# Second attention's last steps: values of the second sample group ahead of the turns, and an output projection begun early

## The reference

```python
outs, lses = [], []
for g, (win, dil) in enumerate(((128, 1), (512, 4), (2048, 16))):   # three dilation groups, 8 heads
    o_g, l_g = dilated(q[:, :, g], k, v, dil, win // dil)
    ...
w = softmax(stack(lses), axis=0)
x = x + sum(w * outs).reshape(..., 512) @ w_o_b
```

## Time and profile before

| what | value |
|---|---|
| median of three runs | 1412.44 us |
| the profiled execution | 1412.59 us |
| its span | 1410.9 us |
| TensorE busy | 1389.5 us (98%) |
| VectorE, ScalarE, POOL busy | 456.2, 325.8, 173.3 us |
| mean granted TensorE clock | 0.998 |

### The profile page before, as it was taken

How to read it: one execution, slowest core, us unless ns; L and a number is a source line. 1 busy time by engine, 2 the same in 40 slices (tenths; PEclk the granted TensorE clock), 3 DMA queues, 4 the chain that set the end, 5 groups by cost and what they waited for, 6 DMA issues and landing times.

```text
span 1410.9 us, 35332 instructions
## 1 busy us (share of the span) xinstructions
PE 1389.5 (98%) x16009; PEld 841.7 (60%) x16009; DVE 456.2 (32%) x964; ACT 325.8 (23%) x629; POOL 173.3 (12%) x218
## 2 busy tenths in 40 slices
PE   9999999999999899999999999999999999999997
PEld 7885999999998573353353353353354354344344
DVE  7967666664587541120120120120120120120111
ACT  6446544344453642001001001001001001001000
POOL 5623320000165611000000000000000000000100
PEclk9999999999999999999999999999999999999999
DMA  8959795535755378999999999999999999999993
GB/s 268 317 171 318 253 360 181 158 109 164 252 179 190 112 301 352 408 418 418 410 418 420 407 418 419 410 418 420 407 418 419 408 419 420 409 419 419 401 420 144
DMA packets 146427, 471.62 MB, mean 334 GB/s; under 512 B 9760, under 2 KB 81824, under 8 KB 117472
## 3 DMA queue, kind: packets, MB, share of 16 engines
q1 hardware_dynamic: 138544, 439.48, 79.6%
q0 software_dynamic: 7728, 29.82, 5.8%
HBM read 451.17 MB, written 18.09 MB: 333 GB/s over the span
## 4 chain that ended last, share of the span: by engine, by line
PE 95%; DVE 2%; ACT 1%; issue 1%; DMA 1%; SPq 0%; DVEq 0%; ACTq 0%
PE psum L1220 41%; PE psum L1260 21%; PE psum L367 9%; PE psum L368 9%; PE psum L369 9%; PE psum L929 1%; PE psum L993 1%; PE psum L865 1%; PE psum L914 1%; PE psum L954 1%; DMA raw<-in_w_qkv_a 1%; PE psum L972 1%; DVE p_b L1697 0%; PE psum L856 0%; PE psum L1204 0%
## 5 line engine op out<-in xcount | busy, mean ns | idle before, releaser
L1220 PE MATMUL psum<-wexp,xg 128*32 128x512 f32 (+1 forms) x6144 | 579.2, 539 | 0.0
L1220 PEld LDWEIGHTS psum<-wexp,xg 128*32 128x32 f32 x6144 | 199.4, 110 | 374.8 <-issue 373.3
L1260 PE MATMUL psum<-wexp,act 128*32 128x256 f32 x5376 | 291.5, 379 | 0.0
L2063 DVE TENSOR_TENSOR am<-sg,psum 128x512 f32<-128x512 f32 (+1 forms) x48 | 26.9, 616 | 731.7 <-issue 485.2
L1260 PEld LDWEIGHTS psum<-wexp,act 128*32 128x32 f32 x5376 | 174.8, 110 | 117.0 <-issue 3.1
L367 PE MATMUL psum<-hh,whi 128*128 128x288 f32 x696 | 207.4, 298 | 0.0
L368 PE MATMUL psum<-hl,whi 128*128 128x288 f32 x696 | 205.4, 295 | 0.0
L369 PE MATMUL psum<-hh,wlo 128*128 128x288 f32 x696 | 205.1, 295 | 0.0
L363 DVE TENSOR_TENSOR wlo<-raw,whi 128x2048 fp32r<-128x2048 f32 (+1 forms) x66 | 144.6, 2192 | 54.4 <-ACT whi L359 54.3
L367 PEld LDWEIGHTS psum<-hh,whi 128*128 128x128 f32 x696 | 130.9, 188 | 8.5 <-issue 8.3
L368 PEld LDWEIGHTS psum<-hl,whi 128*128 128x128 f32 x696 | 130.9, 188 | 0.1
(11 more groups left out here) (304 smaller groups left out, 1052.3 us busy)
## 6 DMA issues: line engine op xcount, KB each, us to landing
wexp<-in_w_moe SPq DMA_DIRECT2D x224, 1024.0 KB, 11.6
wexp<-in_w_moe SPq DMA_DIRECT2D x128, 768.0 KB, 10.8
raw<-in_w_gu_dense SPq DMA_DIRECT2D x22, 1024.0 KB, 5.6
wexp<-in_w_moe SPq DMA_DIRECT2D x32, 512.0 KB, 12.6
raw<-in_w_qkv_a SPq DMA_DIRECT2D x12, 1024.0 KB, 12.8
raw<-in_w_down_dense SPq DMA_DIRECT2D x16, 704.0 KB, 4.5
raw<-in_w_q_b SPq DMA_DIRECT2D x6, 1024.0 KB, 5.0
h_rows<-zeros POOLq DMA_DIRECT2D x14, 384.0 KB, 10.1
```

The costliest lines, as they stand in the source:

```text
L1220: ins = nc.tensor.matmul(ps[NG * part + r][32 * j:32 * j + 32, 0:wd], xg[:, r, 32 * k:32 * k + 32], wexp[:, q % RING, wd * j:wd * j + wd], ...
L1260: ins = nc.tensor.matmul(ps[6 + r // 2][32 * j:32 * j + 32, 256 * (r % 2):256 * (r % 2) + 256], act[:, r, 32 * kk:32 * kk + 32], wexp[:, q ...
L2063: V.tensor_tensor(am[:, r, 0:wd], sg[:, r, 0:wd], ps[NG + r][:, 0:wd], ALU.mult).then_inc(sem("gated_up"), 1)
```

## The change

For layer B alone (layer A's calls give the same order as before). On TensorE, step t = 6 becomes: S1's values, turn 6, turn 7, S1's pick, then the products of tiles 0 to 2 over pairs 0 and 1. Step t = 7 becomes: turn 8, P2's values, turn 9, then the products of tiles 0 to 2 over pair 2. Step t = 8 keeps P3's values, and `residual` afterwards makes pair 3 of tiles 0 to 2 and all of tiles 3 to 7. ScalarE scales S1's result in front of the copies of jobs 6 and 7 and takes the high part behind them, all at t = 6. VectorE takes S1's low part at t = 6, behind the low part of P1 and in front of job 9's probabilities, where it had stood behind them.

```diff
@@ TensorE, attend @@
                     if t == n and ng == 1:
-                        residual(P_WO, tiles_wo, "wo", b, True)
+                        residual(P_WO, tiles_wo, "wo", b, (0, nj - 4))
                     kind1, i1 = unit_at(b, t - lag)
+                    kind2, i2 = unit_at(b, t - lag - 1)
+                    if ng > 1 and t == n:
+                        sample_values(jobs_of(b, t - lag - 1)[0], i2)
+                        for k in jobs_of(b, t - lag):
+                            turn_probs(k, kind1)
+                        pick_rows(i2)
+                        residual(P_WOB, tiles_wob, "wob", b, (0, nj - 2))
+                        continue
...
-                    if kind3 == S_:
+                    if kind3 == S_ and (ng == 1 or t < n):
                         pick_rows(i3)
                     for k in jobs_of(b, t - lag)[1:2]:
                         turn_probs(k, kind1)
+                    if ng > 1 and t == n + 1:
+                        residual(P_WOB, tiles_wob, "wob", b, (nj - 2, nj - 1))
@@ TensorE, residual @@
-                first = 4 * (groups - 1)
-                for m in range(2) if early else range(KD):
-                    if early:
+                ahead, first = (2, kn - 4) if b is A else (3, kn - 1)
+                for m in range(ahead) if early else range(KD):
+                    if early and b is A:
                         eng.wait_ge(sem(f"exped_{tg}"), ...)
+                    elif early:
+                        eng.wait_ge(sem(f"masked_{tg}"), max(masked_place(...) ... if score_bank(b, k, g) == m))
...
-                    for k in range(first) if early else range(first if m < 2 else 0, kn):
+                    for k in range(*early) if early else range(first if m < ahead else 0, kn):
                         if m == 0:
                             eng.wait_ge(sem(f"o_low_{tg}"), k + 1)
                             eng.wait_ge(sem(f"so_copied_{tg}"), groups + k // 4 + 1)
@@ ScalarE, attend @@
+                        kind3, i3 = unit_at(b, t - 3)
+                        if t == len(b["units"]):
+                            scale_out(i3)
+                            for k in before:
+                                copy_job(k)
+                            sample_high(i3)
+                            continue
...
-                        if kind4 == S_:
+                        if kind4 == S_ and t < len(b["units"]):
                             sample_high(i4)
@@ VectorE, attend @@
                                 if k == b["vector_adds"][0] and low[0] == P_:
                                     prompt_low(low[1])
+                                    sample_low(unit_at(b, t - 3)[1])
...
-                        if kind4 == S_:
+                        if kind4 == S_ and t < len(b["units"]):
                             sample_low(i4)
```

## The result

The changed kernel took 1419.9 us (median of five runs, 1416.82 to 1420.33), the kernel before 1412.49 us beside it: ratio 1.0043, 95% interval 1.0029 to 1.0057. So it is slower by about 6 us (7.4 by the medians), beyond the forecast of 1415.0 and beyond its range (1412.3 to 1417.2). A second set of twelve runs gave 1416.63 us against 1412.95: 1.0030 (1.0016 to 1.0043). The profiled execution belongs to the first set (1420.29 us, span 1418.6; before 1412.59 and 1410.9).

The account below looks back on a forecast made before the run. TensorE was taken to bound the kernel. Idle +1.79, turns +0.44, two restarts 2 x 0.10 and small-step spacing 0.19 summed to 2.62 us, giving 1415.0 us; range 1412.3 to 1417.2.

Parts of the forecast that it names:

- 1.: S1's values, put in front of turn 6 on TensorE, start no earlier than before, at 492.55.
- 2.: Turns 6 and 7 behind S1's values: starts 495.93 and 497.51, low clock over turn 6 only, +0.44 us.
- 3.: S1's pick, then a new TensorE wait of 0.84 us for VectorE's low part; 2.1 us of cover remain before turn 9.
- 4.: First 18 early products on TensorE: 0.23 us plus 2.48, ending at 501.56, with no wait on the scores.
- 5.: Turn 8, P2's values, turn 9, then 0.59 us idle before pair 2's 9 products, which start at 503.90.
- 6.: Rest of the projection: 1.03 us idle before pair 3, start at 507.09, last product ending at 517.29.
- The price without a drop: If S1's values run at full clock, they and turn 6 end 1.15 + 0.38 us earlier; the sum falls to about 1.1.
- the clock term of the sum: TensorE's clock is low over S1's values and turn 6, then full from turn 7, whose next start comes after 0.45 us.
- rival C: TensorE's clock drops a second time behind 497, over the 18 products: 2.4 us more, +5.0 in all, 1417.4 us; chance 0.15.
- Rivals B and D: B: early products cover two 0.67 us waits, at most -1.34, chance 0.11. D: first expert's weight wait hides delay, 1412.4, chance 0.08.

Follow-up runs that it names:

- g1: The changed kernel again with no edit, twelve runs on another chip: 1.0030 of the kernel before.
- e1: The changed kernel plus 24 products with overwritten results in TensorE's wait ahead of S1's values: 26.86 us from S0's pick to the last product's end, at full clock.
- e4: The changed kernel with the 9 products of pair 2 moved behind P3's values: 1416.0 us.
- f4: The changed kernel plus overwritten products behind S1's values, 5 behind turn 6 and 6 behind the pick, the wait in front left: 1415.57 us.
- e3: The changed kernel without the early projection, which is whole again behind P3's values: times from 1411.82 to 1420.24 us.
- g2: The kernel before with turn 6 also waiting for the low part of S0's result, the order behind kept: time as before, clock 0.9969.

## Why the prediction was wrong

The sum was right and the case was not. In g1's profile, where the clock dropped once as forecast, the stage takes 517.58 - 489.27 = 28.31 us, 2.71 more than before; the forecast was 2.62. Shifted by 0.20 to the start of before's pick, its steps stand beside the forecast as follows.

1. S1's values at 492.56 (492.55). Right: the move brought them no earlier.
2. Turn 6 at 495.90 (495.93), turn 7 at 497.47 (497.51). Right.
3. First early product at 499.04 (499.08), idle 0.78 (0.84), released by VectorE's low part. Right, as was the cover on VectorE's side: turn 9 never waited for job 9.
4. Turn 8, behind the 18 products, at 501.49 (501.56). Right.
5. Pair 2 at 503.95 (503.90), idle 0.69 (0.59). Right.
6. Pair 3 at 507.20 (507.09), idle 1.01 (1.03). Right.

The price without a drop holds as well: the order was then to cost 1.1 over before as profiled, and e1 gives 26.86 - 25.60 = 1.26.

What failed is the clock term of the sum. Step 2 had the clock back at its full level from turn 7 on ("the other now runs at the full clock"), as in before, and all that might come on top was "If it drops a second time behind 497, half speed on the 18 products costs 2.4 more", which was given 0.15 as rival C. In the changed kernel's profile the clock does not drop a second time, it doesn't rise: it is low over S1's values, both turns, the pick, the 18 products and turn 8. Rival C's own form, two drops, occurs as well, in e4's profile. Counted from S0's pick and against g1, that is 0.81 at S1's values, 0.36 at turn 7, 2.00 at the products (501.24 to 505.69 = 4.45 against 2.45), 0.36 at turn 8, and 0.04 between: 3.57, and 2.71 + 3.57 = 6.28. Of the changed kernel's 17 runs 10 had a mean clock of 0.995 or below, against 14 of the 108 of before. That clock counts drops in other parts too, so it is only an estimate of how often this one is long: not a case of 0.15, but of about half. The range was too narrow by the same term; its upper end lay 0.2 below rival C's own time of 1417.4, and the profiled execution with the long low clock took 1420.29.

The argument against C had been that the stretch from 498 to 500 of before held only 1.43 us of work in 2 and kept 1.00. But there the clock had risen already, by 497, behind turn 7. Gaps behind a clock that is still low are another thing: f4, which only fills them, has the clock of before.

The rule of the Trainium skill that was weighed ("TensorE: Matmul & The Clock Gate", section "Why this matters for your kernels": no idle gaps between bursts) pointed the right way, but the gap alone does not decide here, and the measurement counts. The gap of before, 2.62 us, is shorter than those that the Trainium skill warns of there, and the clock fell behind it, so the trace agreed with less of the rule than the prediction said; e3's and g2's profiles have gaps of 3.20 and 3.16 us and no drop. And the length of the gap does not tell how long a drop lasts (3.6 us in g1's profile and 13.7 in the changed kernel's, both with the same 3.20), which made most of the loss. Rivals B and D fell: the waits arose as forecast, and nothing behind the projection hid the delay: in g1's profile the first expert starts 2.91 us later than before, which is the stage's 2.71 and the 0.20 ahead of it.

What stays open: why the same program's clock drops in one execution and not in the next. No run here shows it; only how often it happens was moved. The traces show no more than that the clock fell at different places of the same program, inside the wait (changed) or 0.8 us behind the start of S1's values (g1).

## What to carry to other kernels

Before moving work out of a wait, find the event that ends the wait: if it doesn't come earlier, whatever had run inside the wait goes onto the path. A wait of TensorE near a clock drop had a second price here, which depended on how dense the work behind it was; bound it by half speed over everything up to the next dense stretch, and give that case real weight: here it was on in about half the executions. Where differences are tenths of a per cent, list the granted clock of every run beside its time, and compare at equal clock.

## What the runs showed of the hardware that was not expected

- Useless work did not cost time and probably saved some: 20 overwritten products in a wait of 2.6 us raised the mean clock from 0.997 to 0.9986. The median went from 1413.25 to 1411.64 us, but the interval holds 1 (0.9994, 0.9985 to 1.0003); with the early projection, over two sets, it is 0.9991 (0.9983 to 0.9998).
- Most of this kernel's scatter goes with the clock: the 29 runs of before beside e1 to e4 reach from 1410.71 us at 1.000 to 1417.45 at 0.994, and the linear fit on the clock takes up about three quarters of their variance.
- The same wait of 3.20 us was followed by no drop (e3), by one of 3.6 us (g1), by two with full clock between them (e4), and by 13.7 us in one piece (changed). In g1 the clock rose at 497.2 in the middle of a wait, behind S1's values and turn 6; in the changed kernel it rose behind 5.2 us of work without a gap (501.24 to 506.4).
